# A twelfth row buffer in exchange for the fifth weight slot, in a kernel that mixes attention with gathered experts

## What is computed

```python
xn = _rmsnorm(x, mix_norm_w[l])
proj = xn @ w_in[l]                       # diff attention, GLA, memory attention, gates
...
merged = (g[:, :, 0] * (o_da @ w_br_da[l]) + g[:, :, 1] * (o_gla @ w_br_gla[l])
          + g[:, :, 2] * (o_xa @ w_br_xa[l]))
x = x + merged @ w_out[l]
x = x + _peer(_rmsnorm(x, ffn_norm_w[l]), peer_w_q[l], ...)

def _peer(xn, w_q, sub_keys, expert_u, expert_v):
    q = (xb @ w_q).reshape(T, H, 2, PEER_QDIM // 2)
    s = jnp.einsum('thpc,pnc->thpn', q, sub_keys)
    top_s, top_i = lax.top_k(s, K)        # 16 of 128 keys on each side
    best_s, best_j = lax.top_k(cand_s, K) # 16 of the 256 sums
    g = jax.nn.softmax(best_s, axis=-1)
    u, v = expert_u[idx], expert_v[idx]
    act = gelu(jnp.einsum('thkd,td->thk', u, xb))
    return jnp.einsum('thk,thkd->td', g * act, v)
```

## Time and profile before

| | us |
|---|---|
| median of three runs | 3633.49 |
| lowest and highest | 3623.59, 3634.26 |
| the profiled execution | 3634.84 |
| its span, first to last instruction | 3633.0 |
| TensorE's matmuls busy | 2843.4 (78%) |
| VectorE busy | 2214.6 (61%) |
| GpSimd busy | 1154.4 (32%) |
| ScalarE busy | 690.8 (19%) |
| bytes moved | 1304.05 MB, mean 359 GB/s |

### The profile page before, as it was taken

One profiled execution on the slowest core, in us unless ns is written; L12 is line 12 of the kernel. 1 busy time (PEld: TensorE's weight loads), 2 busy tenths in 40 slices (PEclk: granted clock), 3 DMA queues, 4 the chain that ended last, 5 costly groups with the idle time before them and its releaser, 6 DMA issues. The chain is left out here.

```text
span 3633.0 us, 31949 instructions
## 1 busy us (share of the span) xinstructions
PE 2843.4 (78%) x11208; PEld 1447.6 (40%) x11208; DVE 2214.6 (61%) x5619; ACT 690.8 (19%) x1255; POOL 1154.4 (32%) x1036
## 2 busy tenths in 40 slices
PE   8889867899987857799988867798988835555555
PEld 3568632355645413355645322345653501111111
DVE  1231277875554886875554887775554787666665
ACT  2230113621111113622111112531111000000000
POOL 0000013433332333433332233343332334444442
PEclk9999988899998978999998878899998968777777
DMA  5324559999999999999999999999999959999998
GB/s 166 107 93 151 174 194 408 393 423 409 418 425 371 401 387 361 391 386 409 418 425 374 386 398 369 369 367 412 418 425 410 414 227 399 427 427 421 427 427 350
DMA packets 212016, 1304.05 MB, mean 359 GB/s; under 512 B 25216, under 2 KB 25744, under 8 KB 80272
## 3 DMA queue, kind: packets, MB, share of 16 engines
q0 software_dynamic: 148608, 1078.00, 72.3%
q1 hardware_dynamic: 63248, 224.01, 16.8%
HBM read 1288.28 MB, written 13.63 MB: 358 GB/s over the span
## 5 line engine op out<-in xcount | busy, mean ns | idle before, releaser
L626 POOL DMA_INDIRECT rowbuf<-in_peer_uv,idx x884 | 987.7, 1117 | 2204.8 <-PE acc L923 1522.6
L923 PE MATMUL acc<-rowbuf,diag 128*64 128x512 f32 x3536 | 1069.4, 703 | 406.0 <-DVE diag L1602 397.7
L1592 DVE CUSTOM_DVE_ANT_0 rowbuf<-rowbuf,xr 128x1024 f32<-128x1024 f32 x884 | 1058.2, 1220 | 273.3 <-DMA rowbuf<-in_peer_uv,idx 269.5
L923 PEld LDWEIGHTS acc<-rowbuf,diag 128*64 128x64 f32 x3536 | 260.4, 154 | 1023.1 <-DVE diag L1602 530.1
L1192 ACT ACTIVATE acts<-dots 128x2 f32<-128x2 f32 x512 | 104.1, 203 | 2249.3 <-DVE dots L1592 2175.5
L1602 DVE TENSOR_SCALAR diag<-consts,acts,gw 128x64 f32<-128x64 f32 x1024 | 287.8, 344 | 291.4 <-ACT acts L1192 122.8
L675 PE MATMUL bank<-xnT,W 128*128 128x256 f32 x1600 | 366.8, 385 | 0.0
L675 PEld LDWEIGHTS bank<-xnT,W 128*128 128x128 f32 x1600 | 300.5, 191 | 87.3 <-issue 48.7
L661 PE MATMUL bank<-W,xnT 128*128 128x512 f32 x736 | 334.1, 604 | 0.5 <-ACT kv L978 0.5
L675 PE MATMUL bank<-arena,W 128*128 128x256 f32 x1024 | 245.4, 398 | 57.5 <-DMA W<-in_w_blocks 56.4
L923 PE MATMUL acc<-kv,diag 128*64 128x512 f32 x440 | 192.9, 758 | 90.4 <-DVE diag L1602 86.7
(11 more groups left out here) (190 smaller groups left out, 2394.2 us busy)
## 6 DMA issues: line engine op xcount, KB each, us to landing
W<-in_w_blocks SPq DMA_DIRECT2D x360, 512.0 KB
rowbuf<-in_peer_uv,idx POOLq DMA_INDIRECT x884
xs<-in_x SPq DMA_DIRECT2D x16, 512.0 KB
xr<-x SPq DMA_DIRECT2D x32, 256.0 KB
out_y<-xs SPq DMA_DIRECT2D x8, 512.0 KB
x<-arena SPq DMA_DIRECT2D x8, 512.0 KB
out_y<-xr POOLq DMA_DIRECT2D x8, 512.0 KB
xs<-memory SPq DMA_DIRECT2D x3, 1024.0 KB, 8.9
```

Source lines behind the costliest of these rows:

```text
L626: pool.indirect_dma_start(rows[SLOT[g]], None, a["peer_uv"], bass.IndirectOffsetOnAxis(ap=idx[:, at // NB, at % NB:at % NB + 1], axis=0)). ...
L923: mm = pe.matmul(acc[HP * j:HP * (j + 1), h * HALF:(h + 1) * HALF], diag[:, c % DIAGS, j, :], v[:, D + h * HALF:D + (h + 1) * HALF], start ...
L1592: dve.tensor_tensor_reduce(out=u, in0=u, in1=xr[:, t, j, :], scale=1.0, scalar=0.0, op0=ALU.mult, op1=ALU.add, accum_out=dots[:, c % QS, j ...
```

## The change

Two constants change. The rest follows from them.

```diff
@@ -174,7 +174,7 @@
-W_SLOTS = 5
+W_SLOTS = 4
 W_AT = {(job, part): i for i, (_, _, job, (_, part)) in enumerate(W_BLOCKS)}
@@ -207,7 +207,7 @@
 DIAGS, QS = 3, 4
-ROWS = 11
+ROWS = 12
 KV_ROWS, KV_UNTIL = 4, 184
 EXTRA = W_SLOTS // 2 + KV_ROWS
```

## The result

| | us |
|---|---|
| changed kernel, median of 20 runs | 3637.04 (3625.69 to 3645.54) |
| kernel before, median of 20 runs beside it | 3633.22 (3623.59 to 3639.29) |
| ratio | 1.0015, 95% interval 1.0009 to 1.0022 |
| the profiled execution of the changed kernel | 3633.89, its span 3632.1 |

The forecast was 3628, some 6 us less than before; the kernel came out about 5 us above. The time lies in the stated range (3609 to 3645) and within 0.3% of before, but on the other side of it. A second measurement, in a later session, gave 1.0021 (1.0012 to 1.0030).

What follows compares the result with a forecast made beforehand. TensorE bounds it to about 545 us, then full DMA beside busy TensorE or VectorE, from 2974 us gather bytes. Profiled 3634.8 minus 6 (buffer 6, slot 0) is 3629; the runs' median, 1.35 lower, gives 3628; range 3609 to 3645.

Steps and rivals of the forecast that it cites:

- the sum: Twelfth buffer's gain: 2.0 us at step 3's scores, 1.0 at step 4's state update, 2.5 in its merge, 0.3 at 2864.88.
- the margins of 6.4 and 7.6 us: Spare time for a regular weight block with four slots: 6.4 us without gathers, 7.6 or more in mixed stretches; cost nothing.
- the irregular places: Where SyncE takes up weights behind stores of x and loads of x and residual rows; lost slot's cost there 0.
- Four slots don't delay that first block: First weight block behind SyncE's other transfers is issued late because of their order, long after slots came free; cost 0.
- The bound of 22 us: Most the lost slot could cost: one block's 3.72 us in each of six places where SyncE has other transfers.
- Even 16.28 us is just under 16.5: A weight block's 16.28 us in the chain, at 2795.57 us, still fits three blocks' time in a mixed stretch, 16.5.
- the transfer of 8.9 us: Landing time of 1024 KB, two weight blocks, under full gathers; a single block was put between 4.1 and 8.9 us.
- While DMA is full, an earlier issue only makes the queue longer: Twelfth buffer's earlier gathers gain nothing where DMA is full; a loss from this buffer was excluded.
- My sign of what would be wrong: VectorE's 139.5 us falling by a third, or the last step starting 20 us earlier or more, would mean rival A.
- rival A: DMA bounds everything after 545 us, so extra gathers fill dips: 23 us gained (3610) or 47 (3587); chance 0.21.
- Rival B: Weights come one block time late at six places behind SyncE's other transfers: 22 us slower, 3656; chance 0.09.
- C: Rival: wherever gathers are queued, transfers are limited by rate, not buffers, so no gain: 3633.5; chance 0.05.

## Why the prediction was wrong

**What held.** The last step is nearly a constant: from the issue of its first gather to the end it is 662 to 665 us in all 20 profiles, with 16, 17 or 18 buffers. So nearly all of the differences come from before that. The twelfth buffer was worth about what the sum said, 5.8 us, once the waits behind xr were short: 5 us with the gathers held, 8 and 4 us with the weights ahead. With SyncE's order as it is in this change it gave 4 us and 0. Its places were partly right: near 2030 us the copy gained 1.6 us (2.0 forecast), the gap of 3.16 us at the state update is 1.58 now, so also 1.6 (1.0 forecast); in the merge of step 4 only 0.85 us of the 2.5. No regular weight block came late, as the margins of 6.4 and 7.6 us said.

**The step that failed** is the sentence on the irregular places: "Four slots don't delay that first block", with the price of nothing for the lost slot. It measures about 8 us, and 0 to 2 us once those blocks go ahead of xr; so the price is in the waits behind xr. I had looked at when the slots come free, and they do come free long before. I had not looked at what shares the DMA engines with the block. TensorE's waits behind xr last as long as SyncE's seven or so MB need, plus the gathers that land meanwhile; with a slot less, up to three more gathers land in that stage, two on average in step 3. The bound of 22 us had the right places, but its mechanism was wrong: in the same six places TensorE waits, and only longer.

The reading beside it was too narrow as well. "Even 16.28 us is just under 16.5" takes the block of step 4. In the same profile the same block took 24.9 us in step 2 (issued at 1105.3) and 24.3 us in step 3 (issued at 1922.7), well over three blocks' time, behind the loads of xr and beside the gathers. The price of a block under the shared queues was in the trace; the transfer of 8.9 us that I took for it had nothing of its own queue ahead of it.

**The same step hid the buffer's own side effect.** "While DMA is full, an earlier issue only makes the queue longer" isn't harmless if another queue's transfer is on the path: by the end of step 3's WQ stage 454, 455 and 456 gathers have been issued with ten, eleven and twelve buffers. With ten buffers and five slots the stage of step 3 was 43.8 us and the waits for weights were 37.4 us, against 52.2 on average with eleven. From eleven to twelve, in the old order, the difference isn't resolved: 59.3 and 60.2 us of waits with eleven, 59.7 and 60.7 with twelve.

**My sign of what would be wrong was half right.** I wrote that VectorE's 139.5 us falling by a third, and a last step that starts 20 us earlier, would speak for rival A. They fell by 30%, and the last step started 3.8 us earlier. VectorE's waiting for gathers isn't time on the path one for one, and that its fall gave so little speaks against A. So does the kernel with ten buffers, where it rose by 103 us, to 242.9, for a price of 10 us.

**Rival B** had the right sign, and the slot cost a third of its price. C, as an account of the whole, is out, since a buffer does gain (10 us from ten to eleven). But its idea of a lower rate holds in places that the prediction had not looked at: DMA moves 424 to 427 GB/s in most full stretches, and about 300 at full busy shares while xr lands.

**What stays open.** The runs show that the price nearly goes when the weights don't stand behind xr. That more gathers land in the WQ stage with four slots is clear in step 3 only, and even there single profiles overlap (13.4 MB with five slots, 13.1 with four). Why a slot less does this isn't shown. One link is in the traces: with five slots SyncE issues its last weight block before the stores of x 26.7 us ahead of them, with four 21.2 and with three 15.7, in each of steps 2 to 4 and in all ten profiles with SyncE's order of the change and no hold. So each slot less puts SyncE one block's 5.5 us less ahead when the stage begins. But one block is 1.23 us of DMA by itself, and the stage is unstable even with five slots (48.3 to 53.6 us in step 3), so how this becomes 8 us isn't settled. The lengths of the stage by step rest on three and four profiles. Nor is it shown why the rate falls while xr lands.

## What to carry to other kernels

When two queues share full DMA engines, a buffer more on the one may not be free: look which of the other queue's transfers the compute engines wait for, and count what the first queue moves in that time. Ask of a prefetch slot not only whether the next block lands in time, but how much of the needed bytes is in when the DMA gets full and other queues take their share. Before adding buffers, take the transfers that nobody needs soon out of the way of those that are waited for: here an exchange of two lines was worth 8 to 9 us, more than the twelfth buffer, and made the trade of slot for buffer pay. And check the rate where the engines are full: a busy share of 1 isn't always the full rate.

## What the runs showed of the hardware

With gathers queued, SyncE's queue got a little over a third of the DMA engines' time (39.5% and 34.8% in two stretches). Its blocks of 0.524 MB then landed 3.7 us apart (1905.4, 1909.2, 1912.9 and 1916.6 us with four slots used of five), where the full rate of 427 GB/s would give 1.23. With the gathers held, the first four of WQ's second half landed at 1924.3, 1925.6, 1926.9 and 1928.1.

While the loads of xr (64 partitions each, where those of x and of the weights have 128) land beside gathers, the DMA engines are full at some 300 GB/s: 299 at a share of 1.02 from 1110 to 1120 us in the kernel before, 277 at 1.01 from 1970 to 1980 us with the weights ahead. With the gathers held they move 216 to 255 GB/s in the stretch where these loads land.

Of the 16 us between two executions of the kernel before, one of them only moved by 4 KB (spans of 3617.8 and 3633.9 us), 10 us are in TensorE's waits for weights (44.9 and 55.2 us).
